# Expert weights in half matrices, and the row gather and block sum moved ahead of the weights' wait

## The reference: what is computed

```python
def moe_ffn(h, router_w, router_b, w_gate, w_up, w_down):
    ...
    def expert_block(args):
        xi, e = args
        return (jax.nn.silu(xi @ w_gate[e]) * (xi @ w_up[e])) @ w_down[e]
    yb = lax.map(expert_block, (xb, block_expert)).reshape(n_blocks * MOE_BLK, d)
    return jax.ops.segment_sum(yb * slot_w[:, None], slot_tok, num_segments=n + 1)[:n]
```

## Time and profile before

| what | value |
|---|---|
| median of three executions | 1610.53 us |
| profiled execution | 1607.88 us, its span 1606.0 us |
| PE busy | 1269.3 us (79%) |
| DVE, ACT busy | 600.4 us (37%), 386.9 us (24%) |
| data moved | 507.68 MB, mean 316 GB/s |
| experts' stage of layer 0 | about 410 to 871 us of the span |
| experts' stage of layer 1 | about 1159 us to the end |

### The profile page before, as it was taken

One profiled execution on the slowest core, in us unless ns is written; L12 is line 12 of the kernel. 1 busy time (PEld: TensorE's weight loads), 2 busy tenths in 40 slices (PEclk: granted clock), 3 DMA queues, 4 the chain that ended last, 5 costly groups with the idle time before them and its releaser, 6 DMA issues. The chain is left out here.

```text
span 1606.0 us, 36189 instructions
## 1 busy us (share of the span) xinstructions
PE 1269.3 (79%) x14878; PEld 730.8 (46%) x14879; DVE 600.4 (37%) x1637; ACT 386.9 (24%) x812; POOL 35.3 (2%) x79
## 2 busy tenths in 40 slices
PE   4898888986799987768854699878799987666665
PEld 3355555543465554434422547634355543332332
DVE  1538564436322221211111556775544333122212
ACT  1254224213132232222211322543211111101110
POOL 0201101000000000000001000000000000000000
PEclk8999898998899999988987699979799998888888
DMA  8610997537899999999996520065689999999996
GB/s 318 230 70 22 347 370 260 189 158 301 345 414 428 428 429 429 428 430 429 429 428 262 191 105 0 1 269 201 262 331 427 426 428 428 428 428 429 428 428 287
DMA packets 81810, 507.68 MB, mean 316 GB/s; under 512 B 13293, under 2 KB 17746, under 8 KB 56394
## 3 DMA queue, kind: packets, MB, share of 16 engines
q1 hardware_dynamic: 74712, 489.21, 74.2%
q10 hardware_dynamic: 3906, 8.83, 1.4%
q0 software_dynamic: 3120, 8.63, 1.4%
HBM read 494.61 MB, written 12.03 MB: 315 GB/s over the span
## 5 line engine op out<-in xcount | busy, mean ns | idle before, releaser
L1618 PE MATMUL bank<-sb_ring,sb_scratch 128*32 128x256 f32 x2240 | 141.5, 409 | 54.7 <-DMA sb_ring<-in_moe_w_up 45.7
L1800 PE MATMUL bank<-sb_ring,sb_scratch 128*32 128x256 f32 x1664 | 122.0, 457 | 70.6 <-DMA sb_ring<-in_moe_w_up 66.6
L1699 DVE TENSOR_TENSOR sb_scratch<-sb_scratch,bank 128x128 f32<-128x128 f32 x50 | 14.4, 288 | 323.2 <-ACT sb_scratch L1652 323.2
L1618 PEld LDWEIGHTS bank<-sb_ring,sb_scratch 128*32 128x32 f32 x2240 | 76.6, 118 | 117.6 <-issue 78.4
L1800 PEld LDWEIGHTS bank<-sb_ring,sb_scratch 128*32 128x32 f32 x1664 | 66.4, 130 | 125.0 <-issue 104.3
L1656 ACT ACTIVATE sb_scratch<-bank 32x256 f32<-32x256 f32 x200 | 74.9, 374 | 162.1 <-PE bank L1628 160.4
L1880 DVE TENSOR_TENSOR sb_scratch<-sb_scratch,bank 128x128 f32<-128x128 f32 x38 | 10.9, 288 | 250.1 <-ACT sb_scratch L1836 250.1
L1598 PE MATMUL bank<-sb_h,sb_scratch 128*32 128x256 f32 x1632 | 99.2, 384 | 3.3 <-DVE sb_scratch L1686 3.3
L1836 ACT ACTIVATE sb_scratch<-bank 128x128 f32<-128x128 f32 x38 | 10.5, 277 | 374.1 <-PE bank L1800 374.1
L1618 PE MATMUL bank<-sb_scratch 128*32 128x256 f32 x960 | 61.6, 414 | 24.6 <-DMA sb_scratch<-in_moe_w_up 22.0
L1800 PE MATMUL bank<-sb_scratch 128*32 128x256 f32 x768 | 53.7, 442 | 30.6 <-DMA sb_scratch<-in_moe_w_up 28.8
(11 more groups left out here) (400 smaller groups left out, 1870.3 us busy)
## 6 DMA issues: line engine op xcount, KB each, us to landing
sb_ring<-in_moe_w_gate SPq DMA_DIRECT2D x44, 2048.0 KB, 27.4
sb_ring<-in_moe_w_up SPq DMA_DIRECT2D x44, 2048.0 KB, 31.9
sb_ring<-in_moe_w_down SPq DMA_DIRECT2D x41, 2048.0 KB, 34.3
sb_ring<-in_ada_w SPq DMA_DIRECT2D x21, 2048.0 KB, 16.3
sb_scratch<-in_moe_w_gate SPq DMA_DIRECT2D x20, 2048.0 KB, 28.8
sb_scratch<-in_moe_w_up SPq DMA_DIRECT2D x20, 2048.0 KB, 32.2
sb_scratch<-in_moe_w_down SPq DMA_DIRECT2D x20, 2048.0 KB, 33.9
sb_ring<-in_cd_w_in SPq DMA_DIRECT2D x4, 2048.0 KB, 9.4
```

What stands on the lines that cost most here:

```text
L1618: last = nc.tensor.matmul(c.bank(1, 2, FQ)[MB * q:MB * q + MB, :, :], m.xt[:, k, :], m.gu[j][:, :, k, q * FQ:(q + 1) * FQ], start=k == 0, ...
L1699: v.tensor_tensor(m.hm, m.sg, c.ps[1][:, FQ:2 * FQ], ALU.mult).then_inc(hm_ready, 1)
L1800: last = nc.tensor.matmul(c.bank(1, 2, FQ)[MB * q:MB * q + MB, :, :], m.xt[:, k, :], m.gu[j][:, :, k, q * FQ:(q + 1) * FQ], start=k == 0, ...
```

## The change

Four things change in the code. Every 2 MB matrix is loaded as two transfers of 1 MB (per partition 8 KB in place of 16 KB) in the order gate first half, up first half, gate second half, up second half, down first half, down second half, each half with a semaphore of its own. A slot's first gate/up half is given back as soon as the product over its four k-steps is done (`gu_first`). In PE's block, `gather` (and in layer 1 `add_block`) stand ahead of the wait for the gate/up weights, where they stood between the gate/up product and the down product; in layer 1 their order is also swapped. In layer 1 `refill_down` loads the downs of places 6 and 7 as soon as places 0 and 1 have used theirs. The semaphores for all this are freed on GpSimd's queue in `mla_stage` (one more instruction).

```diff
-def mla_stage(c, m, md):
+def mla_stage(c, m, md, used):
...
+            nc.clear_and_free_semaphores(used)
...
-        self.gu_in = [c.sem(f"gate_up_in{j}") for j in range(RING)]
-        self.down_in = [c.sem(f"down_in{j}") for j in range(RING)]
-        self.semaphores = [self.small_in, self.rows_in, self.gate_in, *self.gu_in, *self.down_in]
+        self.gu_in, self.down_in = ([[c.sem(f"{name}_{half}_in{j}") for half in ("first", "second")] for j in range(RING)] for name in ("gate_up", "down"))
+        self.semaphores = [self.small_in, self.rows_in, self.gate_in, *(x for slot in self.gu_in + self.down_in for x in slot)]
...
-        self.spare_down = {RING + a: (place, c.sem(f"spare_down_in{a}")) for a, place in enumerate(places[:1 + layer])}
-        self.semaphores += [done for _, done in self.spare_down.values()]
+        self.spare_down = {RING + a: (place, [c.sem(f"spare_down_{half}_in{a}") for half in ("first", "second")]) for a, place in enumerate(places[:1 + layer])}
+        self.semaphores += [x for _, done in self.spare_down.values() for x in done]
...
-def load_matrix(c, m, sp, e, j, name):
+def load_half(c, m, sp, e, j, name, half):
 
     at = slice(e, e + 1) if isinstance(e, int) else bass.ds(e, 1)
     if name == "moe_w_down":
-        dst, src, done = m.down[j], c.i[name].rearrange("l e (p k) n -> l p e (k n)", k=DE // P), m.down_in[j]
+        dst, k, done = m.down[j], DE // P, m.down_in[j][half]
     else:
-        dst, src, done = m.gu[j][:, int(name == "moe_w_up")], c.i[name].rearrange("l e (p k) n -> l p e (k n)", k=KC), m.gu_in[j]
-    sp.dma_start(dst.rearrange("p k n -> p (k n)"), src[m.layer][:, at, :].rearrange("p e n -> p (e n)")).then_inc(done, 16)
+        dst, k, done = m.gu[j][:, int(name == "moe_w_up")], KC, m.gu_in[j][half]
+    n = dst.shape[2]
+    src = c.i[name].rearrange("l e (p k) n -> l p e (k n)", k=k)[m.layer][:, at, half * k // 2 * n:(half + 1) * k // 2 * n]
+    sp.dma_start(dst[:, half * k // 2:(half + 1) * k // 2, :].rearrange("p k n -> p (k n)"), src.rearrange("p e n -> p (e n)")).then_inc(done, 16)
+
+
+def load_matrix(c, m, sp, e, j, name):
+    for half in range(2):
+        load_half(c, m, sp, e, j, name, half)
...
+def load_gate_up_half(c, m, sp, e, j, half):
+    load_half(c, m, sp, e, j, "moe_w_gate", half)
+    load_half(c, m, sp, e, j, "moe_w_up", half)
 
 
 def load_gate_up(c, m, sp, e, j):
-    load_matrix(c, m, sp, e, j, "moe_w_gate")
-    load_matrix(c, m, sp, e, j, "moe_w_up")
+    for half in range(2):
+        load_gate_up_half(c, m, sp, e, j, half)
 
...
-                sp.wait_ge(gu_product, end)
-                sp.sem_inc(released, 1)
-                load_gate_up(c, m, sp, e, j)
+                for half in range(2):
+                    sp.wait_ge((gu_first, gu_product)[half], end)
+                    sp.sem_inc(released, 1)
+                    load_gate_up_half(c, m, sp, e, j, half)
                 if isinstance(place, int) and place in spare:
                     return
                 sp.wait_ge(y_product, end)
...
-                    (down, down_in), down_loads = m.spare_down[e], 32
+                    (down, down_in), down_loads = m.spare_down[e], 16
...
                 with pe.Fori(first, end) as b:
-                    pe.wait_ge(m.gu_in[j], rounds * 32 + 32)
                     pe.wait_ge(xt_ready, b + 1)
-                    for k in range(KC):
-                        for q in range(CB):
-                            last = nc.tensor.matmul(c.bank(1, 2, FQ)[MB * q:MB * q + MB, :, :], m.xt[:, k, :],
-                                                    m.gu[j][:, :, k, q * FQ:(q + 1) * FQ], start=k == 0, stop=k == KC - 1)
-                    last.then_inc(gu_product, 1)
                     pe.wait_ge(picked, b + 2)
                     gather()
-                    pe.wait_ge(down_in, down_loads)
+                    for half in range(2):
+                        pe.wait_ge(m.gu_in[j][half], rounds * 32 + 32)
+                        for k in range(half * KC // 2, (half + 1) * KC // 2):
+                            for q in range(CB):
+                                last = nc.tensor.matmul(c.bank(1, 2, FQ)[MB * q:MB * q + MB, :, :], m.xt[:, k, :],
+                                                        m.gu[j][:, :, k, q * FQ:(q + 1) * FQ], start=k == 0, stop=k == KC - 1)
+                        last.then_inc((gu_first, gu_product)[half], 1)
                     pe.wait_ge(hmt_ready, b + 1)
                     pe.wait_ge(y_copied, b + 1)
-                    for k in range(DE // P):
-                        for q in range(CB):
-                            last = nc.tensor.matmul(c.ps[3][MB * q:MB * q + MB, 0:DQ], m.hmt[:, k, :], down[k][:, q * DQ:(q + 1) * DQ],
-                                                    start=k == 0, stop=k == DE // P - 1)
+                    for half in range(2):
+                        pe.wait_ge(down_in[half], down_loads)
+                        for k in range(half * DE // P // 2, (half + 1) * DE // P // 2):
+                            for q in range(CB):
+                                last = nc.tensor.matmul(c.ps[3][MB * q:MB * q + MB, 0:DQ], m.hmt[:, k, :], down[k][:, q * DQ:(q + 1) * DQ],
+                                                        start=k == 0, stop=k == DE // P - 1)
                     last.then_inc(y_product, 1)
...
-                sp.sem_inc(released, 1)
-                load_gate_up(c, m, sp, e, j)
-                if isinstance(place, int) and place in spare:
-                    return
+                for half in range(2):
+                    sp.wait_ge((gu_first, gu_product)[half], end)
+                    sp.sem_inc(released, 1)
+                    load_gate_up_half(c, m, sp, e, j, half)
+
+            def refill_down(place, after, j):
+
+                end = bound(sp, after + 1, 1, last_block)
+                e = bound(sp, place + (NE + 2), 0, NE - 1)
                 sp.wait_ge(y_product, end)
                 sp.sem_inc(released, 1)
                 load_matrix(c, m, sp, e, j, "moe_w_down")
 
-            for j in range(RING):
-                refill(RING + j, j)
-            with sp.Fori(2, ROUNDS) as r:
+            for place in range(RING, 2 * RING):
+                refill(place, place - RING)
+                ahead = place + RING if place in spare else place
+                refill_down(ahead, place - RING, place - RING)
+            for place in range(2 * RING, 3 * RING):
+                refill(place, place - 2 * RING)
+                if place - RING not in spare:
+                    refill_down(place, place - RING, place - 2 * RING)
+            with sp.Fori(3, ROUNDS) as r:
                 for j in range(RING):
                     refill(r * RING + j, j)
+                    refill_down(r * RING + j, (r - 1) * RING + j, j)
             for place in range(ROUNDS * RING, NE):
                 refill(place, place % RING)
+                refill_down(place, place - RING, place % RING)
...
-                    pe.wait_ge(m.gu_in[j], rounds * 32 + 32)
                     pe.wait_ge(xt_ready, b + 1)
-                    for k in range(KC):
-                        for q in range(CB):
-                            last = nc.tensor.matmul(c.bank(1, 2, FQ)[MB * q:MB * q + MB, :, :], m.xt[:, k, :],
-                                                    m.gu[j][:, :, k, q * FQ:(q + 1) * FQ], start=k == 0, stop=k == KC - 1)
-                    last.then_inc(gu_product, 1)
-                    add_block(b + 1, False)
                     pe.wait_ge(picked, b + 2)
                     gather()
-                    pe.wait_ge(down_in, down_loads)
+                    add_block(b + 1, False)
+                    for half in range(2):
...
```

31 lines of the change are left out of this document (19 added, 12 removed).

## The result

| | kernel before | changed kernel |
|---|---|---|
| median of 4 runs, us | 1612.69 (1609.92 to 1618.04) | 1641.30 (1639.23 to 1644.71) |
| profiled execution, us | 1607.88 | 1644.71 |
| its span, us; mean granted clock | 1606.0; 0.906 | 1642.8; 0.922 |

The ratio is 1.0189, with a 95% interval of 1.0163 to 1.0215.

A forecast was written before the change was run, and what follows sets the result against it. Late in a stage the weights' stream sets the pace, but it stalls where PE gives slots back late. Terms 24.1 - 3.3 + 3.1 - 5.0 + 3.1 = +22.0 us on 1607.9, plus 2.6 for a median: 1632 us, range 1619 to 1646.

The forecast's parts named there:

- PE's block: Both layers: PE idles between gate/up and down product once the gather is moved, 1.4 us more per block (1.2 to 1.6).
- half transfers: Both layers, full stream: two halves cost 0 to 0.05 us more per matrix, 0 to 6.2 us, middle taken, +3.1 us.
- Layer 0, early places: Layer 0's first places: later give-backs stall the stream, 11.4 us lost by place 7, then 12.7 us more.
- The cycles: Layer 0 after place 7: three rounds of a three-block and a one-block place, 34.7 us against 30.5 for six matrices, 4.2 lost each.
- Layer 0, the end: Layer 0 behind the last up's landing: work ends about 6.6 us behind instead of 9.9, -3.3 us (1.6 to 3.9 gained).
- half a down product (0.9 to 1.7) follows: Layer 0's last place: after the down's second half lands, only half a product remains, 0.9 to 1.7 us.
- Layer 1: Layer 1 before place 9: PE's later give-backs use up the gain from early down loads, +3.1 us instead of -2.5.
- Layer 1, the end: Layer 1 behind the last up: only the down's second half and half a product remain, -5.0 us (3.2 to 5.5 gained).
- (a): Early places: idle time is shorter than read and the stream stays the bound; with none, -7.5 us, 1603; chance 0.09.
- (b): Whole kernel: no difference, with idle time near 0.6 us per block; chance 0.03.
- (c): PE's clock falls in the new pauses, some 6 us more per block, about 1900 us in all; chance 0.03.
- (d): Weights' stream: each transfer's 3.9 us lag shows over 58 refills with three more transfers, 680 us; chance 0.01.

The follow-up runs named there:

- the later comparison: The unedited changed kernel measured again beside the kernel before, with 4 and 16 runs: 1643.26 us against 1610.97, ratio 1.0207.
- the order alone: Kernel before with only the gather (in layer 1 also the block sum) moved ahead of the gate/up weights' wait, whole matrices: 1640.37 us, ratio 1.0163.
- the order put back: Changed kernel with gather and block sum again between the gate/up and down products, the rest of the change kept: 1605.88 us, ratio 0.9976.
- the sum left between: Kernel before with only the gather moved ahead, in layer 1 only, the block sum staying between the products: 1608.59 us, one execution.
- the halves alone: Changed kernel with gather and block sum back between the products and without layer 1's early down loads: 1613.04 us, ratio 1.0010.
- the parts that gain: Kernel before plus layer 1's early down loads, gate/up of places 3 to 8 and all of place 31 in halves: 1597.64 us, ratio 0.9927.
- quarters: Kernel before with every matrix of the ring in four transfers of 4 KB per partition: 1645.51 us, one execution.

## Why the prediction was right, point by point

It said 1632, between 1619 and 1646, and slower, by a sum of +22.0 us; it was 1641.3 and slower by 28.6 us, and by 32.3 in the later comparison. The mechanism, PE's block in the early places, was right where I had named it. Of the terms, that for the half transfers was much too small; the others were off by less, and in both directions.

- **PE's block** (1.4 us more): shown as the cause by the order alone, the order put back and, in layer 1, the sum left between. The idle time in the rows is 1.15 to 1.25 us, since they let the gate/up product end 3.64 us behind its start, while the next work can start 3.47 us behind it; from block to block it is 1.36 to 1.42 us, and the blocks take 8.27 to 8.90 us, forecast 8.3 to 8.9. The gate of place 7 is issued at 488.84, forecast 488.9.
- **Layer 0, early places** (+24.1 = 11.4 + 12.7): in both traces of the changed kernel the landings are 10.8 us late at place 7 and 21.2 at place 13, 10.4 us more. The cycles themselves came out as forecast: between the gate issues of places 7, 9, 11 and 13 lie 34.7, 34.9 and 35.3 us, forecast 34.7. What fell short is the other side: in the trace before, the landings of places 7 and 9 lie 32.2 us apart and not 30.5, so that the first cycle loses 2.6 us. In the traces with layer 0 unedited place 13 lands 0.3 and 2.3 us sooner than in the trace before, so the 2.9 us that are missing may for the most part be chance.
- **Layer 0, the end** (-3.3): from the last landing on it was -1.7 in the first trace and -3.2 in the second, and -1.2 in a trace with this layer unedited (sum left between). In the first trace the second gate/up half and the whole down product ran at half clock (1.2 GHz), 3.64 us each. In the second, with the same program and the same pause of 1.16 us between them, they ran at full clock but for the last 16 matmuls:

```profile
888.25 1.93 PE L1634 MATMUL bank<-sb_ring,sb_scratch 128*32 128x256 f32 x32 [3.47 <-DMA sb_ring<-in_moe_w_up]
891.34 1.07 PE L1643 MATMUL bank<-sb_ring,sb_scratch 128*32 128x256 f32 x16 [1.16 <-DVE sb_scratch L1716]
893.18 1.94 PE L1643 MATMUL bank<-sb_ring,sb_scratch 128*32 128x256 f32 x16 [0.77 <-DMA sb_ring<-in_moe_w_down]
```

So "half a down product (0.9 to 1.7) follows" failed in one trace (3.64 us of a whole one) and nearly held in the other. That the pause keeps the product behind it slow is not shown: with the order alone the down product behind a pause of 1.21 us took 1.93 us, at full clock. Without the pause, with the halves alone, the order put back and the parts that gain, the end took 3.2 to 3.9 us less than before.
- **Layer 1** (+3.1): place 9 is 2.7 us late in both traces of the changed kernel. With the order alone 7.2; the early downs and the earlier halves take the rest off.
- **Layer 1, the end** (-5.0): -5.3 and -3.4 in the two traces, -4.7 with the halves alone. Right.
- **Half transfers** (+3.1, bounds 0 to 6.2): this is the term that was most wrong. "I take the middle" of 0 and 0.05 us per matrix; it is 0.078 us (0.235 us per expert, three matrices), for 124 matrices 9.7 us. In the changed kernel's landings it shows as 5.2 us from place 9 on in layer 1. In layer 0 they fall back by 6.2 us from place 13 on, of which 18 experts at 0.235 us are 4.2; the other 2.0 us come with the order alone and whole matrices too (24.4 us late at place 13, 26.4 at 31). The rows I took the price from were three landings that stood in another stage behind a whole matrix; their spacing of 2.45 to 2.5 us could not tell 4.90 from 4.98. The Trainium skill ("DMA: Bandwidth & Descriptors", section "Measured") gives 341 GB/s for a 1 MB transfer issued from GpSimd and 425 for one of 16 MB. The trace agrees that the smaller transfer is the slower, and not with the size: halves of 1 MB in a full queue moved 422 GB/s, whole matrices 428.
- With the sizes as the first trace has them, the sum is 21.2 - 1.7 + 2.7 - 5.3 + 11.4 = +28.3 us. This is that trace taken apart, and no test of the terms.
- **Rivals.** (a) and (b) asked for 0.6 us per block or less; it is 1.36 or more, and they fall. (c) fell: the granted clock is 1.00 in the early stretches of the changed kernel shown above, with a pause in every block. Later, where PE waits for weights, it is higher than before: 1.00 from 1300 to 1400 us (with the order alone as well), where the kernel before has 0.86.

```profile
1300.00:1400.00 100.00, 81.22 (x1324) 41.61 (x1320) 33.76 (x107) 15.81 (x21) 0.00 (x0) 1.00 1.01 422
```

The rule on micro-idles of the Trainium skill ("TensorE: Matmul & The Clock Gate", section "A second HAM failure mode: psum-queue depth-cycling") isn't seen in these stretches, with a pause of 1.2 us in each block of some 8.9 us. (d) fell: the stream keeps 422 GB/s with twice the transfers.

Open: whether a piece's price hangs on its size or on the number of transfers, since both changed together in halves and quarters; why the clock at layer 0's end differs between two executions of the same program; the 1.9 us in blocks 3 to 5 with the order alone; and what part, if any, the change has in the middle's 2.5 and 8.3 us.

## What to carry to other kernels

Before work is moved away from between two dependent products, ask what the engine does while the others turn the first product into the second one's input: the moved work was nearly free there, since it filled that wait. A pause costs only where the engine is the one waited for, so look at the places in which the stream stands still, here the first 14 of 32 in layer 0, and care less for the idle time elsewhere. Cutting transfers pays at the ends of a stream, where a half starts work or frees a slot sooner, and costs in its middle; take each part where it gains.
